# The order of the seven products of a down projection, interleaved between output blocks

## The reference

```python
def swiglu_ffn(x, w_gate, w_up, w_down):
    return (jax.nn.silu(x @ w_gate) * (x @ w_up)) @ w_down

x = layer_norm(DEEPNORM_ALPHA * x + 0.5 * swiglu_ffn(x, ...), g, b)
```

## Time and profile before

| | us |
|---|---|
| median of 3 runs | 4681.34 |
| lowest and highest run | 4549.9, 5129.03 |
| the profiled execution | 4549.1 |
| its span on the slowest core (core 7) | 4547.3 |
| its span on the other cores | 4511.4 to 4542.6 |

### The profile page before, as it was taken

How to read it: one execution, slowest core, us unless ns; L and a number is a source line. 1 busy time by engine, 2 the same in 40 slices (tenths; PEclk the granted TensorE clock), 3 DMA queues, 4 the chain that set the end, 5 groups by cost and what they waited for, 6 DMA issues and landing times.

```text
span 4547.3 us, 83656 instructions; the slowest of 8 cores (4511.4 to 4547.3 us)
## 1 busy us (share of the span) xinstructions
PE 4462.1 (98%) x32617; PEld 3110.4 (68%) x32617; DVE 3209.7 (71%) x5681; ACT 1784.7 (39%) x3695; POOL 617.1 (14%) x1170
## 2 busy tenths in 40 slices
PE   9999999999999999999999999999999998999998
PEld 6676676678686666667868666765687665766565
DVE  2386786677777678677777767867777785687746
ACT  2143343334344334333434533533434353254323
POOL 1211111111111111111101111111010111111120
PEclk9999999999999999999999999999999999999999
DMA  7546546455454664654535556466354556556581
GB/s 154 87 71 98 83 68 86 70 80 91 65 87 73 93 87 68 90 77 73 97 60 88 83 87 91 72 78 93 66 89 76 84 85 83 75 83 89 85 143 45
DMA packets 238572, 381.15 MB, mean 84 GB/s; under 512 B 70000, under 2 KB 117104, under 8 KB 238192
## 3 DMA queue, kind: packets, MB, share of 16 engines
q0 software_dynamic: 167904, 329.85, 49.0%
q1 hardware_dynamic: 70288, 45.96, 4.2%
HBM read 683.99 MB, written 21.51 MB: 155 GB/s over the span
## 4 chain that ended last, share of the span: by engine, by line
PE 89%; DMA 6%; DVE 3%; issue 1%; ACT 0%; POOL 0%; SPq 0%; POOLq 0%; ACTq 0%; DVEq 0%
PE bank L568 67%; PE bank L579 22%; DMA ringM<-win 2%; DMA xb<-wd 2%; DMA E<-wd 1%; DMA HM<-wd 1%; DVE HM L608 1%; DVE xs L614 1%; DVE xb L608 1%; DMA ydram<-HM 0%; DVE xs L608 0%; DMA xs<-xin 0%; DVE HM L614 0%; DVE HF L614 0%; DVE E L608 0%
## 5 line engine op out<-in xcount | busy, mean ns | idle before, releaser
L568 PE MATMUL bank<-xb,ringF 128*128 128x352 bf16 (+8 forms) x11376 | 1719.9, 311 | 5.7 <-ACT xb L601 3.7
L568 PEld LDWEIGHTS bank<-xb,ringF 128*128 128x128 bf16 x11376 | 1100.3, 97 | 602.3 <-issue 8.5
L601 ACT ACTIVATE sg<-bank 128x352 f32<-128x352 f32 (+10 forms) x1206 | 537.4, 446 | 1519.1 <-PE bank L568 1318.3
L568 PE MATMUL bank<-xb,ringM 128*128 128x352 bf16 (+8 forms) x4416 | 679.0, 313 | 32.1 <-DMA ringM<-win 32.0
L568 PEld LDWEIGHTS bank<-xb,ringM 128*128 128x128 bf16 x4416 | 427.7, 97 | 270.6 <-issue 35.7
L614 DVE SCALAR_TENSOR_TENSOR HF<-sg,bank 128x352 bf16<-128x352 f32 (+9 forms) x690 | 351.1, 509 | 260.2 <-PE bank L568 234.7
L634 POOL DMA_DIRECT2D ringF<-wgu x488 | 258.2, 529 | 2003.6 <-PE bank L568 1699.7
L614 DVE SCALAR_TENSOR_TENSOR xs<-xs,agb,bank 128x352 f32<-128x352 f32 (+9 forms) x544 | 348.5, 646 | 207.5 <-PE bank L568 107.8
L601 ACT ACTIVATE HM<-xs 128x704 bf16<-128x704 f32 (+8 forms) x286 | 221.2, 787 | 696.3 <-PE bank L579 294.6
L608 DVE TENSOR_TENSOR xs<-xs,HM 128x1408 f32<-128x1408 f32 (+8 forms) x288 | 464.2, 1617 | 7.1 <-ACT HM L601 5.0
L608 DVE TENSOR_TENSOR xs<-xs,bank 128x352 f32<-128x352 f32 (+11 forms) x484 | 267.5, 557 | 221.5 <-PE bank L568 128.8
(11 more groups left out here) (152 smaller groups left out, 4945.7 us busy)
## 6 DMA issues: line engine op xcount, KB each, us to landing
ringF<-wgu POOLq DMA_DIRECT2D x422, 256.0 KB, 5.1
ringM<-win POOLq DMA_DIRECT2D x136, 256.0 KB, 5.8
ringF<-wgu POOLq DMA_DIRECT2D x66, 512.0 KB, 5.7
ringM<-wgu POOLq DMA_DIRECT2D x66, 512.0 KB, 5.6
ringF<-wd POOLq DMA_DIRECT2D x104, 256.0 KB, 4.6
xb<-wd POOLq DMA_DIRECT2D x105, 224.0 KB, 5.2
E<-wd POOLq DMA_DIRECT2D x81, 224.0 KB, 5.8
ringM<-wout POOLq DMA_DIRECT2D x64, 256.0 KB, 4.0
```

The source lines that it names most:

```text
L568: ins = e.matmul(banks_t[b][:, o:o + n], l.ap, r.ap, start=(i == 0), stop=(i == len(prs) - 1))
L601: return p.emit("act", lambda e: e.activation(out=out.ap, in_=in_.ap, func=func, bias=bi, scale=sc), R, [out], dur=k + size_of(out) * 0.00 ...
```

## The change

One list of 28 products takes the place of four times the same seven. Turn 0 runs p1 p2 p5 p6 p3 p7; turns 1 and 2 run p1 p5, then p4 of the turn before, then p6 p3 p2 p7; turn 3 runs p1 p5, p4 of turn 2, p6 p3 p7 p2 p4. The places of the weights are handed on in the new order, with p4 last.

```diff
@@ -1342,10 +1342,12 @@
                 yield Need("dve", w, cond=cond)
                 sP[i].add(tt(operand(i, k, 0, nh), a, b, op, rate=2.0))
 
-        PRODUCTS = [("p1", "a11", "b11", None, (0, 0)), ("p2", "a12", "b21", None, (0, 0)),
-                    ("p6", "s2", "t2", "p1", (0, 1)), ("p5", "s1", "t1", None, (1, 1)),
-                    ("p7", "s3", "t3", "p6", (1, 1)), ("p3", "s4", "b22", "p5", (0, 1)),
-                    ("p4", "a22", "t4", "p7", (1, 0))]
+        PRODUCTS = {"p1": ("a11", "b11", None, (0, 0)), "p2": ("a12", "b21", None, (0, 0)),
+                    "p6": ("s2", "t2", "p1", (0, 1)), "p5": ("s1", "t1", None, (1, 1)),
+                    "p7": ("s3", "t3", "p6", (1, 1)), "p3": ("s4", "b22", "p5", (0, 1)),
+                    "p4": ("a22", "t4", "p7", (1, 0))}
+        TURNS = ["p1 p2 p5 p6 p3 p7", "p1 p5 -p4 p6 p3 p2 p7", "p1 p5 -p4 p6 p3 p2 p7", "p1 p5 -p4 p6 p3 p7 p2 p4"]
+        turns = [(p_ - 1, x[1:]) if x[0] == "-" else (p_, x) for p_ in range(4) for x in TURNS[p_].split()]
         KEPT = ("p1", "p5", "p6", "p7")
         LOADS = ("b11", "b12", "b22", "b21")
         SUMS = (("t1", "b12", "b11"), ("t3", "b22", "b12"), ("t2", "b22", "t1"), ("t4", "b21", "t2"))
@@ -1357,7 +1359,8 @@
                 blk[p_, name], frees[p_, name] = free.pop(0)
                 wP[p_, name] = PromiseN(len(cuts) if name in LOADS and blk[p_, name] >= 5 else 1)
             blk[p_, "t3"], frees[p_, "t3"], wP[p_, "t3"] = blk[p_, "b12"], None, PromiseN(1)
-            free += [(blk[p_, x[2]], (p_, x[0])) for x in PRODUCTS]
+            order_ = TURNS[p_].replace("-p4 ", "").split()
+            free += [(blk[p_, PRODUCTS[x][1]], (p_, x)) for x in order_ + ["p4"] * ("p4" not in order_)]
         said = {None}
         loaded = set()
 
@@ -1463,29 +1466,29 @@
                         bankF.put(b, de)
             return go
 
-        for p_ in range(4):
-            banks = {}
-            for name, a, w, onto, out in PRODUCTS:
-                deps = [wP[p_, w]]
-                deps += [sP[a]] if a in sP else [q for c in range(kh) for q in hP[c + (0 if a == "a11" else kh)]]
-                if onto:
-                    deps.append(banks[onto][1])
-                yield Need("pe", deps, [] if onto else [(pairF, 1) if nt == 2 else (bankF, 1)], prio=f_prio)
-                bs = banks.pop(onto)[0] if onto else pairF.get() if nt == 2 else [bankF.get()]
-                kept = PromiseN(nt) if name in KEPT else None
-                if kept:
-                    banks[name] = bs, kept
-                for t, (o, n) in enumerate(parts):
-                    me = mm_part(bs[t][1], n, [(wblk(blk[p_, w], k, k + 1, lo, *home), operand(a, k, o, n)) for k in range(kh)],
-                                 onto is None, True, onto is not None)
-                S.task(Need("dve", [me], prio=-1), evac(p_, bs, out, kept))
-                st["vtF"] += kh * nh / 2400.0
-                said.add((p_, name))
-                load_ready()
-                if gates and s == 0 and (p_, name) == (2, "p4"):
-                    for k in held:
-                        ringM.load(k)
-                    held.clear()
+        banks = {}
+        for p_, name in turns:
+            a, w, onto, out = PRODUCTS[name]
+            deps = [wP[p_, w]]
+            deps += [sP[a]] if a in sP else [q for c in range(kh) for q in hP[c + (0 if a == "a11" else kh)]]
+            if onto:
+                deps.append(banks[p_, onto][1])
+            yield Need("pe", deps, [] if onto else [(pairF, 1) if nt == 2 else (bankF, 1)], prio=f_prio)
+            bs = banks.pop((p_, onto))[0] if onto else pairF.get() if nt == 2 else [bankF.get()]
+            kept = PromiseN(nt) if name in KEPT else None
+            if kept:
+                banks[p_, name] = bs, kept
+            for t, (o, n) in enumerate(parts):
+                me = mm_part(bs[t][1], n, [(wblk(blk[p_, w], k, k + 1, lo, *home), operand(a, k, o, n)) for k in range(kh)],
+                             onto is None, True, onto is not None)
+            S.task(Need("dve", [me], prio=-1), evac(p_, bs, out, kept))
+            st["vtF"] += kh * nh / 2400.0
+            said.add((p_, name))
+            load_ready()
+            if gates and s == 0 and (p_, name) == (2, "p4"):
+                for k in held:
+                    ringM.load(k)
+                held.clear()
         if st["busy"]:
             st["busy"] = 0
             st["m"] -= 1
```

## The result

| | before | after |
|---|---|---|
| median of 4 runs, us | 4615.62 | 4520.42 |
| lowest run, us | 4546.38 | 4516.08 |
| the profiled execution, us | 4549.1 | 4518.34 |
| its span, slowest core, us | 4547.3 (core 7) | 4516.8 (core 1) |
| ratio, with its 95% interval | | 0.9936 [0.9907, 0.9965] |

The ratio is a gain of about 29 us (16 to 42). The forecast was 4536 within 4511 to 4567, and "within 2%" at 0.95. The time lies in the range and the change is within 2%, but the kernel did get measurably faster, by twice the 13.5 us of the sum and by more than the likeliest case's own range (4527 to 4544).

The account below looks back on a forecast made before the run. PE, busy 98% of the span, was taken as the bound, with 25.9 us of late starts winnable by product order. Terms -17.1 - 2.5 - 4.9 + 9.0 + 2.0 = -13.5 us took 4549.1 to 4536 us, range 4511 to 4567.

Parts of the forecast that it names:

- rival 4: Rest of the program: instructions interleave otherwise and ringM waits move by 10 us or so; 4524 to 4548 or beyond; chance 0.05 beyond the bounds.
- Rival 1: Projection stretches: DVE's queue is laid out anew and all waits but 1.2 us are won; 4524 us; chance 0.12.
- Rival 3: Block 1's p5, 8th product: new wait for weight sum t1 exceeds what is won; up to 4567 us; chance 0.07.
- evacuation waits of blocks 1 and 2: p6, p3, p7 and p4 there follow two other products, hiding late evacuations: 17.1 of 17.2 us go.
- block 0's p6 on s2: Block 0's p6 comes fourth instead of third, so its wait for the last sum s2 goes: minus 2.5 us.
- block 1's p2 on b21: Block 1's p2 moves from 9th to 12th place, so its wait for weight load b21 goes: minus 4.9 us.
- block 1's p5 on t1: Block 1's p5 moves from 11th to 8th place and newly waits for weight sum t1 (b12 - b11): plus 9.0 us.
- block 1's p6 on t2: Block 1's p6, still 10th, may wait for sum t2: plus 2.0 us, the middle of bounds 0 and 4.
- block 0's p7: Block 0's p7 keeps one product between, so its 1.2 us of evacuation waits stay: change 0.
- The loads of later blocks: b22 of blocks 2 and 3 waits for a later product, hidden by 3.6 us of products: cost 0.
- Rival 2: Projection stretches: waits only move, what is won behind is lost in front; 4549 us; chance 0.09.
- Rival 5: PE's matmuls in the stretches: pace improves from 112.5 to 97 ns, worth 73 us; 4476 us; chance 0.01.

Follow-up runs that it names:

- the third chip: Chip of the last four runs: kernel before unchanged, ratio 1.0006; changed kernel unchanged, 0.9941 and 0.9940; changed kernel with weight sums later on DVE's list, 0.9945.
- e4: Kernel before, product order on PE kept; host's modelled weight-load latency 4.5 instead of 2.0 us, so weight sums stand later on DVE's list; ratio 0.9963.
- e3: Against the kernel before: every block runs p1 p5 p6 p3 p7 p2 p4, with one product between those of a chain; ratio 0.9993.

## Why the prediction was right and where it failed

The forecast was half of what was measured, 13.5 us against 29. Some 7 us of the difference are terms of the sum for the stretches, as shown below. The other 8 lie outside the stretches, for which the sum has no term and only rival 4 a word; on the third chip they are all but gone (20 to 24 us of gain). That 4518 lies in the range shows little, since the range was made wide enough for rivals 1 and 3.

By its own terms, in us, as means of the cores, with the range over the three profiles of before and the four of after:

| term of the sum | forecast | measured |
|---|---|---|
| evacuation waits of blocks 1 and 2 | -17.1 | -17.2 to -18.9 |
| block 0's p6 on s2 | -2.5 | -2.5 |
| block 1's p2 on b21 | -4.9 | -1.6 to -3.0 |
| block 1's p5 on t1 | +9.0 | +0.9 to +1.6 |
| block 1's p6 on t2 | +2.0 | 0, and its old 1.8 to 2.1 gone |
| block 0's p7 | 0 (1.2 stay) | 1.4 to 2.0 before, 0.1 to 0.4 after |
| block 0's p3 | none | +1.2 to +1.9 |
| block 1's p1 on b11 | none | +0.9 to +1.6 |
| sum | -13.5 | about -20 |

(The old wait of block 1's p6 is part of the first row, as in the prediction; but more than half of its idle time was for a sum, not for an evacuation. A few stretches in which a matmul's record is missing are left out of this table; the lengths of all stretches give -21.)

**Right: what is lost before and why.** The 25.9 us counted by late starts on core 7, where the idle column had 17.8, is close to the means of all cores in three profiles (25.4, 26.4, 25.8). That count carried the whole argument. The reading of the earlier trace rows, a sum that idles for a load with evacuations behind it, was the cause: e4 removes the waits by moving the sums alone. Two products of cover hide them: after shows none in blocks 1 and 2, where e3 keeps them. The loads of later blocks and the banks cost nothing, as forecast.

**The step that failed: +9.0 for t1 and +2.0 for t2.** The eleven microseconds are 2.4 in the profiles, with p1's share counted in (0.9 to 1.6 for each of the two). Three mis-steps made the difference.
- *Ends of t1 were taken over from the old list of DVE.* In the two stretches with 1.6 us each, for one of them, t1 waited for no load: it ended at 12.5 us because it stood behind the 7th product's evacuation on DVE. Those two terms, 3.2 us, are the same on every core before. After, t1 ends 10.9 us into these two stretches on 10 of the 16 occasions, and on the other six, mostly for its load, 11.1 to 11.8. The two lines of the kernel before, then three from the stretch from 2244.93 of the kernel after, where t1 stands behind the 6th product's evacuation:

```profile
2269.41 0.76 DVE L614 SCALAR_TENSOR_TENSOR xs<-xs,agb,bank 128x528 f32<-128x528 f32 x1 [0.87 <-PE bank L579]
2270.10 0.62 DVE L608 TENSOR_TENSOR HM<-xb 128x896 bf16<-128x896 bf16 x1
```

```profile
2254.58 0.70 DVE L608 TENSOR_TENSOR xs<-xs,bank 128x528 f32<-128x528 f32 x1 [0.87 <-PE bank L579]
2255.20 0.62 DVE L608 TENSOR_TENSOR HM<-xb 128x896 bf16<-128x896 bf16 x1
2256.16 0.76 DVE L614 SCALAR_TENSOR_TENSOR xs<-xs,agb,bank 128x528 f32<-128x528 f32 x1 [0.33 <-PE bank L579]
```

  The row gave it away: no idle time and no load is named at the earlier trace rows's latest sum, so its end was set by its place in the list, which the host lays out anew for the new order.
- *One core was taken for all.* The page's core 7 is the worst of the eight in this. The same formula gives 4.2, 9.0, 4.2, 6.4, 4.5, 4.4, 4.7 and 9.3 us over cores 0 to 7 of that execution, 5.8 in the mean; in the kernel after core 7 itself has 1.6. Its b21 term, 4.9 against a mean of 1.7, came from the same late loads and erred the other way.
- *t2's 2.0 was the middle between bounds.* It came out at the lower one, nothing: two products covered it, as the prediction's own 1.7 against 3.1 us said.

Take 3.2, 3.5 (9.3 less 5.8) and 2.0 from the 11.0, and 2.3 are left, against 2.4 measured. The formula itself held: with the ends that t1 has in the four profiles of after it gives 3.0, 1.9, 2.5 and 1.6 us as means of the cores, and block 1's p1 and p5 together started 3.2, 2.0, 2.7 and 1.7 us late there. What failed is the ends that were put into it.

**Overlooked:** block 1's p1 moves too, from the 8th to the 7th place, and needs b11 from the same run of loads. When these are late it waits first (1.18 us in the stretch shown, 2.28 in the one from 900.89), and p5's wait is the shorter for it. Likewise block 0's p3 and p7 keep one product between, as the prediction says, but p3 now comes before p7; it took over the wait that was to stay with p7. Both moves can be read from the diff.

**The rivals.** Rival 1, all of it won at 4524, was the nearest (4518.3) to the first pair, with the help of what was won outside the stretches; it had 0.12, held down by the t1 term. Rival 2, the waits only move, falls: after has 5 us where before has 25. Rival 3, slower by t1, falls: the 8th product's wait is 0.1 us per stretch, not 1.63. Rival 4, the rest shifts, is partly there: ringM's waits did move by 16 us between the two pages, as the earlier trace rows warned they could, but on the third chip they are alike for both kernels. The lists of work outside the stretches did not change. Rival 5 falls: a stretch without a wait takes 44.27 us, 112.5 ns a matmul, as before. The Trainium skill (TensorE: Matmul & The Clock Gate, Step-by-step: what each phase is for) gives a matmul behind another its columns at 2.4 GHz and about 2.5 ns; an estimate from it for 264 columns is 112.5 ns, and the trace agrees.

**The signs named.** Seen as forecast: no wait of PE for a b21 load, xs L614 under 4 us, the stretch that took 48.70 us shorter by 2.6, an idle 8th product where loads are late, 112.5 ns a matmul, and no stretch over 49 us. Less than forecast: the stretch that took 46.75 us is 0.4 us shorter where 0.5 to 1.5 was named, and the 8th product is 0.56 and 0.70 us idle in two stretches, not about 1. Of the signs against, one was seen in the first pair: ringM waits that move more than all else. Profiles of that pair alone would have put a third of the gain in the wrong place.

**The chances.** 2% was given as about what a measurement of this kernel can tell from no change. The interval came out at 0.3% to either side, so a gain of 29 us can be told, and was.

The Trainium skill (Perfetto Trace Analysis, Optimizing Tensor Performance) says that independent matmul groups should rotate through banks, so that one group's evacuation overlaps the next group's matmuls. The traces agree, and show what the number of groups between is worth where the products of a chain share a bank: 80.9 us lost with none before p4, 22.3 with one everywhere, 5 with two in the middle blocks. The second step is due to what else stands on the evacuating engine's queue, as e4 shows.

## What to carry to other kernels

Count late starts, not idle time, and ask for each what stands ahead of the releaser on its own queue: a 0.7 us evacuation with a product of 1.57 us to cover it is still late behind an instruction that waits for a load. Then there are two cures, more cover on the engine that waits (21 us here) or another order on the engine that is late (15 us with one number of the host's model), and together they leave 2 us. When the times of the old trace are carried over to a new order, separate ends that a transfer sets from ends that a place in a list sets, and take the size of a term from all cores, not from the one on the page.

## What the runs showed of the hardware

In some stretches TensorE's clock fell for a short time with a long wait. The windows of the first and second stretch on core 1 of the run with no product between:

```profile
219.80:271.11 51.31, 48.18 (x396) 0.97 0.46 65
560.56:606.58 46.02, 44.45 (x396) 1.00 0.49 72
```

and PE's timeline around the wait:

```profile
229.43 0.52 PE L579 MATMUL bank<-HM,E 128*128 128x278 bf16 x3
233.08 1.09 PE L579 MATMUL bank<-HF,xb 128*128 128x280 bf16 x4 [3.13 <-DVE xs L608]
...
236.00 0.64 PE L579 MATMUL bank<-HF,xb 128*128 128x280 bf16 x4
```

PE had been at full pace, idled 3.13 us, and the four matmuls behind the idle time show 1.09 us where four later ones show 0.64: they ran at the lower of the two levels, 1.2 GHz, until shortly before 236.0. So this wait cost more than itself, about 1.3 us more over some 14 matmuls (the starts at 233.08 and 236.00 lie 2.92 us apart, and 14 x 0.119 are 1.67).

It is not so after each wait of such a length. On core 3 of the same run four matmuls behind 3.32 us idle show their full pace, 0.61 us for 264 columns:

```profile
2839.74 0.61 PE L579 MATMUL bank<-HF,xb 128*128 128x264 bf16 x4 [3.32 <-DVE xs L608]
```

Other runs show it too. In the kernel before it is three stretches, on cores 1, 3 and 5, each with a late start of 2.3 to 2.4 us; this is the one on core 3, which took 49.96 us:

```profile
2486.91:2536.87 49.96, 46.73 (x396) 0.97 0.52 77
```

Over the stretches of all 14 profiles there are 42 late starts of more than 2 us, and the granted clock fell with 19 of them; in the stretch from 900.89 of the kernel after, with 2.28 us idle, it stayed at 1.00. What tells the 19 from the others, none of the runs shows.
